# Conditioning sums of a fused two-block kernel: products on GpSimd, a folding tree and weight remainders on VectorE

## The reference

```
mod = silu(c) @ ada_w + ada_b                      # c: 1x1024, ada_w: 1024x6144
sh_t, sc_t, g_t, sh_c, sc_c, g_c = split(mod, 6)   # 1024 columns each
h = rms_norm(x, tm_pre_g) * (1 + sc_t) + sh_t
branches = four mixers of h (mLSTM, gated linear attention, convolution module, short convolution)
merged = sum over b of sigmoid(h @ w_gate_b + bias_b) * (branch_b @ w_out_b)
x = x + g_t * rms_norm(merged @ w_o, tm_post_g)
h = rms_norm(x, cm_pre_g) * (1 + sc_c) + sh_c
x = x + g_c * rms_norm(conv_ffn(h), cm_post_g)
```

## Time and profile before

| | |
|---|---|
| three executions | 1868.55, 1870.16, 1872.58 us (median 1870.16) |
| span of the profiled execution, first to last instruction | 1862.2 us |
| around the span (median less span; the profile lists no total of its own) | 8.0 us |
| PE busy | 1752.2 us, 94% of the span |
| DVE busy | 900.6 us, 48% |
| ACT busy | 662.8 us, 36% |
| POOL busy | 421.5 us, 23% |
| mean granted clock of PE | 0.944 of full |
| the stage of gate0 to wo | 472 to 657 us |

### The profile page before, as it was taken

One profiled execution on the slowest core, in us unless ns is written; L12 is line 12 of the kernel. 1 busy time (PEld: TensorE's weight loads), 2 busy tenths in 40 slices (PEclk: granted clock), 3 DMA queues, 4 the chain that ended last, 5 costly groups with the idle time before them and its releaser, 6 DMA issues.

```text
span 1862.2 us, 20099 instructions
## 1 busy us (share of the span) xinstructions
PE 1752.2 (94%) x7716; PEld 1379.7 (74%) x7716; DVE 900.6 (48%) x1193; ACT 662.8 (36%) x794; POOL 421.5 (23%) x152
## 2 busy tenths in 40 slices
PE   6897999999998979999999799999998999999997
PEld 4676667877877748888888478777767688888886
DVE  4559215332789464444433375385444244444323
ACT  2341215323313254454322432243343355454222
POOL 0347202411433401111100045533203211111000
PEclk8898779977999989999999999999999999999999
DMA  8231202210656213333322122222202233332321
GB/s 291 77 93 46 67 24 68 91 46 23 218 176 216 70 44 100 103 90 90 113 90 91 62 68 91 75 69 70 66 24 68 79 91 90 93 109 90 113 90 45
DMA packets 190956, 168.60 MB, mean 91 GB/s; under 512 B 9157, under 2 KB 180717, under 8 KB 190765
## 3 DMA queue, kind: packets, MB, share of 16 engines
q1 hardware_dynamic: 173485, 148.49, 25.9%
q10 hardware_dynamic: 16800, 16.83, 2.8%
q0 software_dynamic: 608, 2.41, 0.3%
HBM read 165.61 MB, written 2.10 MB: 90 GB/s over the span
## 4 chain that ended last, share of the span: by engine, by line
PE 81%; DVE 12%; issue 2%; ACT 2%; SPq 1%; DMA 1%; POOL 0%; DVEq 0%; ACTq 0%
PE bank L1091 22%; PE bank L1093 22%; PE bank L1092 22%; DVE work L1564 4%; DVE work L1627 2%; PE bank L1173 2%; PE bank L1316 1%; DVE tbuf L1536 1%; PE bank L1116 1%; DVE h_lo L1542 1%; SPq L235 1%; PE bank L1236 1%; PE bank L1449 1%; PE bank L1157 1%; PE bank L1227 1%
## 5 line engine op out<-in xcount | busy, mean ns | idle before, releaser
L1091 PE MATMUL bank<-h_hi,w_hi 128*128 128x512 f32 x1536 | 617.0, 402 | 30.1 <-DVE h_lo L1542 23.9
L1092 PE MATMUL bank<-h_lo,w_hi 128*128 128x512 f32 x1536 | 605.8, 394 | 0.0
L1093 PE MATMUL bank<-h_hi,w_lo 128*128 128x512 f32 x1536 | 605.5, 394 | 0.0
L573 POOL TENSOR_TENSOR w_lo<-w_raw,w_hi 128x2048 fp32r<-128x2048 f32 x63 | 326.1, 5177 | 551.9 <-ACT w_hi L648 551.7
L1091 PEld LDWEIGHTS bank<-h_hi,w_hi 128*128 128x128 f32 x1536 | 293.6, 191 | 114.7 <-issue 35.4
L648 ACT ACTIVATE w_hi<-w_raw 128x2048 fp32r<-128x2048 f32 x131 | 250.3, 1911 | 311.1 <-PE bank L1093 241.0
L1093 PEld LDWEIGHTS bank<-h_hi,w_lo 128*128 128x128 f32 x1536 | 293.2, 191 | 62.6
L1092 PEld LDWEIGHTS bank<-h_lo,w_hi 128*128 128x128 f32 x1536 | 293.9, 191 | 60.5 <-issue 1.7
L1524 DVE TENSOR_TENSOR w_lo<-w_raw,w_hi 128x2048 fp32r<-128x2048 f32 x68 | 156.8, 2306 | 252.5 <-ACT w_hi L648 252.5
L1091 PE MATMUL bank<-y_hi,w_hi 128*128 128x512 f32 x480 | 192.1, 400 | 11.2 <-DVE tbuf L1747 8.4
L1897 DVE SCALAR_TENSOR_TENSOR work<-bank,par,work 128x510 f32<-128x510 f32 (+1 forms) x176 | 123.5, 744 | 142.1 <-ACT work L933 142.1
(11 more groups left out here) (223 smaller groups left out, 1534.4 us busy)
## 6 DMA issues: line engine op xcount, KB each, us to landing
w_raw<-in_w_in SPq DMA_DIRECT2D x94, 512.0 KB, 4.6
w_raw<-in_ffn_w_up SPq DMA_DIRECT2D x44, 512.0 KB, 4.6
w_raw<-in_w_up SPq DMA_DIRECT2D x44, 512.0 KB, 4.6
work<-in_ada_w ACTq DMA_DIRECT2D x16, 1024.0 KB, 7.5
w_raw<-in_ffn_w_down SPq DMA_DIRECT2D x22, 512.0 KB, 4.0
w_raw<-in_w_down SPq DMA_DIRECT2D x22, 512.0 KB, 3.7
work<-in_ada_w SPq DMA_DIRECT2D x8, 1024.0 KB, 12.1
w_raw<-in_w_o SPq DMA_DIRECT2D x8, 512.0 KB, 4.1
```

Source lines behind the costliest of these rows:

```text
L573: pool.tensor_tensor(w_lo[u % 2][:, :], raw[u % 2][:, :], w_hi[u % 2][:, :].bitcast(FP32), ALU.subtract)\
L1091: pe.matmul(dst, w_hi[s][:, at:at + n], hi, start=first, stop=False)
L1092: pe.matmul(dst, w_hi[s][:, at:at + n], lo, start=False, stop=False)
L1093: return pe.matmul(dst, w_lo[s][:, at:at + n], hi, start=False, stop=last)
```

## The change

POOL makes `lo` only up to gate0's first unit. After that it gets a new task, `ada_weigh(n)` for blocks 8 to 23: one multiplication in place of the whole block of 128 x 8 x 256 by `c_act`, broadcast over the 256 columns. It waits only for the block's load. Each `ada_sum` on DVE is replaced by `ada_fold(n)`: three additions in place, of 1024, 512 and 256 elements per partition, each linked to the one before. DVE also takes over `lo` for the 14 units from gate0's second to `up1`, at fixed places between the folds. Loads, ACT's list and PE's list are not changed.

```diff
@@ POOL
-            for u in range(U["y2"], U["up1"] + 1):
+            for u in range(U["y2"], U["gate0"] + 1):
                 lo(u)
+            def ada_weigh(n):
+                unit = ada_place(n)
+                pool.wait_ge(sem(f"ada_in{n % 8}"), 16 * (n // 8 + 1))
+                pool.tensor_tensor(unit[:, :, :], unit[:, :, :], c_act.unsqueeze(2).broadcast_to([P, KT, 2 * P]), ALU.mult)\
+                    .then_inc(sem("ada_weighed"), 1)
+            for n in range(8, 24):
+                ada_weigh(n)
@@ DVE
-            for n in range(8, 14):
-                ada_sum(n, ada_place(n))
+            def ada_fold(n):
+                unit = ada_place(n)
+                dve.wait_ge(sem("ada_weighed"), n - 7)
+                ch.link(dve.tensor_tensor(unit[:, 0:4, :], unit[:, 0:4, :], unit[:, 4:8, :], ALU.add))
+                ch.link(dve.tensor_tensor(unit[:, 0:2, :], unit[:, 0:2, :], unit[:, 2:4, :], ALU.add))
+                dve.tensor_tensor(unit[:, 0, :], unit[:, 0, :], unit[:, 1, :], ALU.add).then_inc(sem("ada_summed"), 1)
+            for c in range(4):
+                lo(U["gate0"] + c + 1)
+                if c:
+                    for n in (6 + 2 * c, 7 + 2 * c):
+                        ada_fold(n)
+            lo(U["gate1"])
             gated("y0")
-            for n in range(14, 22):
-                ada_sum(n, ada_place(n))
+            for c in range(4):
+                lo(U["gate1"] + c + 1)
+                for n in (14 + 2 * c, 15 + 2 * c):
+                    ada_fold(n)
+            lo(U["wo"])
             gated("y1")
@@ DVE, after merged_lo
             merged_lo()
+            lo(U["wo"] + 1)
             for n in (22, 23):
-                ada_sum(n, ada_place(n))
+                ada_fold(n)
+            for c in range(1, 4):
+                lo(U["wo"] + c + 1)
             ada_out(T["ada1"][0], 2 * KT, 4 * KT)
```

## The result

The changed kernel takes 1883.5 us (median of four, 1881.72 to 1886.49), the kernel before 1869.36 on the same chip (1868.35 to 1872.58). The ratio is 1.0074, with a 95% interval of 1.0059 to 1.0089: slower by 14 us. The forecast was 1897, slower by 27, in a range of 1876 to 1912. The direction and the mechanism were right, the size was twice too large.

What follows compares the result with a forecast made beforehand. PE, busy 94% of the span, was taken as the bound, with DVE and POOL taking turns at SBUF. 1862.2 (span) + 8.0 (median less span) + 27 (16W - 38.3, W = 4.1) = 1897 us, range 1876 to 1912.

Steps and rivals of the forecast that it cites:

- What bounds the kernel; taking turns: PE bounds, busy 94%; DVE instructions reading SBUF twice and POOL's SBUF readers alternate, a held sum taking 7.83 against 3.61 us.
- The price W: Shared turn held by one POOL weigh of a block: 4.1 us, bounds 3.6 and 4.6.
- 16 x 3.6 - 38.3: Whole budget at the lower weigh price, 16 weighs less 38.3 us saved: +19.3 us; at the chosen price +27.3.
- First piece: Up to `gated("y0")`: six weighs, six folds and three `lo` replace 36.3 us of DVE sums, +9.6 us.
- Last piece: Before `wo`: weighs 22 and 23 hold DVE's remaining additions, two weighs, +8.2 us.
- The middle piece: From `gated("y0")` to `gated("y1")`: eight weighs, eight folds and five `lo` replace 54.0 us, +9.5 us.
- Where it shows first: At gate0's fourth unit: its `lo` stands behind held folds until 514.6, so PE waits some 9 us.
- The signs: Expected in the trace: `gated("y0")` at about 537 or later, `wo` near 631, PE waiting for `w_lo` and `ada_summed`.
- Rival A: Faster: weighs run beside DVE's work, pauses before `gated` go, about -15 us, 1855 us; chance 0.11.
- Rival C: Worse: late turned blocks delay loads four blocks later, +8 to 12 us on top, 1907 us; chance 0.18.
- Rival B: No change: weighs fall where DVE waits for loads or reads PSUM, over 20 us overlap, 1872 us; chance 0.11.
- 8.0 around the span: Median less profiled span of the kernel before, 8.0 us, added to the span of 1862.2 us.

Runs made afterwards that it cites:

- without a weigh: Changed kernel with POOL's multiplication left out, POOL only passing the signal on: 1853.0 us, 0.9936 of the kernel before.
- six fills: Changed kernel with each POOL weigh replaced by six linked fills of an unused area, which read nothing: 1858.8 us, 0.9920 of the kernel before.
- the second trace: The changed kernel run once more with nothing altered: 1884.6 us, 1.0064 of the kernel before.
- the kernel with the remainder first: Changed kernel with `lo` of gate0's fourth unit, `y0` and gate1's first each ahead of its pair of folds: 1890.4 us, 1.0098 of before.
- the last two orders tried: Changed kernel with three `lo` ahead of their folds (1890.4 us), and changed kernel with each weigh cut into two instructions of 1024 elements (1882.2 us).
- one half of this one: Against the kernel before, only `lo` from gate0's second unit on moved to DVE, sums left whole on DVE: 1852.4 us, 0.9932.
- the other costs 25: Against the kernel before, only the sums changed to weigh and fold, all `lo` left on POOL: 1892.4 us, 1.0142.
- the kernel with only the later remainders moved: Kernel before with `lo` from gate0's second unit on moved to DVE, sums unchanged: 1852.4 us (0.9932), again 1854.0 us (0.9945).

## Why the prediction came out as it did

*What bounds the kernel; taking turns.* Right: the holds are as long as foreseen (4.61 us for an addition of 1.22), a waiting addition gets its turn between two weighs (weighs 10 and 11 above), and multiplies from PSUM were not held (0.68 us for the one at 616.05, while a weigh ran). The kernels without a weigh and with six fills show the cause rather than argue it.

*The price W: the mis-sized term.* I took 4.1 us between 3.6 and 4.6. A weigh alone takes 3.60 (7.17 for a pair). The lower estimate was right: the fixed part from L607 and L573, the slope from L591, the instruction with the same broadcast. The middle had nothing for it but that it was four short instructions with four fixed parts. 16 x 0.5 = 8 of the 12.8 us that the forecast was too high.

*The rest, 16 x 3.6 - 38.3 = 19.3 against 14.5: turns taken as back to back.* First piece: +6.6 forecast, +2.8 measured. The first block landed in 5.4 us, 497.13 less 491.69 where ACT issued it, against 7.3 before, and about 2 us of turns overlapped. Last piece: 7.2 forecast, 4.7 measured, since a weigh also runs beside `gated`'s reads of PSUM. The middle piece was 5.5 forecast and 7.3 measured. As the second trace has +4.2 and +5.1 for the first two pieces, their split is no firmer than 2 us; their sum is 12.1 forecast, 10.1 and 9.3 measured. The middle piece holds seven us in which DVE waited for the rounding of gate1's third unit (559.7 to 566.7): a budget that takes every turn as back to back leaves such gaps out, on both sides of the difference.

*Fold and remainder.* Right: 2.33 (without its links) and 2.28 us for 2.4 and 2.3; the 0.42 for 256 elements is exact.

*Where it shows first.* Right in place, too large in size: PE waits for gate0's fourth remainder, 3.7 us of idle time where I had some 9, and 2.7 at gate1's fourth, the only other wait of this kind.

*The signs.* Not all of them came out. `gated("y0")` at "about 537 or later" was met, at 538.08, by luck: the whole stage started 7.9 us later for another reason, and without that it would be 530.2. `wo` started at 626.29, 14.7 us later within the stage, not 27. And PE never waited for `ada_summed` in this trace, where I had such waits at the end of each gate unit; the second trace has one, of 3.4 us.

*Rival A.* Its price was about right (-15 forecast; the stage is 12.6 us shorter than before without weighs and 11 with six fills), its condition false. *Rival C* fits only the kernel with the remainder first. *Rival B* needed an overlap of over 20 us; there were some 5.

*The total.* "8.0 around the span" was not a property of the execution. The changed kernel's profiled execution took 1884.88 us with a span of 1883.1, 1.8 around it. The one of before must have been some 6 us faster than the median, if it had the same 1.8. The sum was a difference on the median, so no harm came of it.

## What to carry to other kernels

When GpSimd and VectorE share a stage, add up the times of their instructions that read SBUF (twice, on VectorE), as if one engine did them all; where VectorE is what PE waits for, a helper on GpSimd pays only if it takes less held time than it saves. Such a sum gave the right sign and here a third too much. It does not rank two orders of the same instructions: for the last two orders tried it missed by 6 to 7 us, once each way, as it leaves out what waits behind each turn. Here a remainder costs 2.3 us on VectorE and 4.6 on GpSimd, and a whole sum 3.9 on VectorE against 3.6 + 2.3 when split, so the best plan of those tried gives GpSimd nothing in this stage. Test a change of two parts one part at a time: one half of this one is worth 12 us, the other costs 25.

## What the runs showed that I had not expected

**The same instructions in the same order come out two ways.** At the filter taps (60 multiply-adds on DVE) GpSimd's remainders get in between, or starve. POOL's timelines of the kernel before and of the changed one, which has the same code there:

```profile
139.34 15.45 POOL L573 TENSOR_TENSOR w_lo<-w_raw,w_hi 128x2048 fp32r<-128x2048 f32 x2 [4.86 <-ACT w_hi L648]
165.49 24.00 POOL L573 TENSOR_TENSOR w_lo<-w_raw,w_hi 128x2048 fp32r<-128x2048 f32 x1 [10.69 <-ACT w_hi L648]
```

```profile
139.77 4.83 POOL L573 TENSOR_TENSOR w_lo<-w_raw,w_hi 128x2048 fp32r<-128x2048 f32 x1 [4.82 <-ACT w_hi L658]
150.65 5.09 POOL L573 TENSOR_TENSOR w_lo<-w_raw,w_hi 128x2048 fp32r<-128x2048 f32 x1 [6.04 <-ACT w_hi L658]
161.72 4.96 POOL L573 TENSOR_TENSOR w_lo<-w_raw,w_hi 128x2048 fp32r<-128x2048 f32 x1 [5.98 <-ACT w_hi L658]
```

In the first the taps end at 185.1 us, in the second at 190.4. That is 5 of the 8 us by which the two stages start apart. Every trace of a kernel with this code shows one or the other. In the table's groups it is the first in all four traces beside 1864.7 us, the second in all four beside 1871.0, and the first in the one beside 1864.6. So within a group it did not change from kernel to kernel, and something that lasts for a while may settle it rather than each execution; what that is was not tried.

**Another part goes with PE's clock.** The two profiles of the kernel with only the later remainders have the same taps, yet `gated("y2")` starts at 459.64 in one and 465.84 in the other. From 200 to 280 us PE was granted a mean of 0.81 of full speed in the first and 0.73 in the second, a different mix of its two levels (1.2 and 2.4 GHz). PE was busy for all of the 80 us in both, and 0.08 of them is 6.4 us, about the 6.2 by which the stages start apart; these are their windows:

```profile
200.00:280.00 80.00, 80.00 (x282) 54.55 (x280) 14.61 (x29) 14.51 (x22) 12.65 (x3) 0.81 0.13 40
```

```profile
200.00:280.00 80.00, 80.00 (x262) 54.70 (x261) 12.82 (x29) 14.01 (x21) 13.18 (x3) 0.73 0.13 40
```

What tips it was not tried. For the kernel before and the changed one this stretch shows hardly a difference (0.77 and 0.76); from 280 to 360 us it is 0.96 and 0.92, and whether that is the rest of their 8 us is not shown. All this is why the stage, which repeats to 0.4 us or better, was a better ruler here than the total.
